# The residual stream kept by tokens: output and down projections into token tiles, norm sums along the free axis

## The chip, the cores and the metric

One core of one Trainium2 chip runs the kernel. The metric is the device time in microseconds (us); smaller is better. PE is TensorE, ACT ScalarE, DVE VectorE, POOL GpSimd and SP the engine that issues most of the DMAs.

## The reference

Two transformer blocks, one after the other, for one sequence of 256 tokens and 1024 features, all in float32. Cut to what the change touches:

```python
# first block
h = rms_norm(x, norm_mix_pre)
...                                   # attention and convolution of h @ w_in
mixed = g_a * y_a + g_c * y_c
x = x + rms_norm(mixed @ w_out, norm_mix_post)
h = rms_norm(x, norm_ffn_pre)
u = conv3(h @ w_up)                   # 1024 -> 2 x 2816
x = x + rms_norm((gelu(u_gate) * u_val) @ w_down, norm_ffn_post)
# second block
x = x + 0.5 * (silu(n @ w1) * (n @ w3)) @ w2      # n = rms_norm(x, ffn1_norm)
x = x + (gate_a * y_a + gate_b * y_b) @ w_out     # mixers of rms_norm(x, mix_norm) @ w_in
x = x + 0.5 * (silu(n @ w1) * (n @ w3)) @ w2      # n = rms_norm(x, ffn2_norm)
return rms_norm(x, final_norm)
```

rms_norm divides each token's 1024 features by the root of their mean square plus 1e-6 and multiplies them by a gain per feature.

## The kernel before

**Weight chunks.** All weight matrices are read once, in 172 chunks of 128 x 2048 floats (1 MB). A ring of three slots holds a chunk three times: raw as SP's DMA lands it, w_hi (ACT's rounding of raw to the format that PE multiplies in one pass, L1294) and w_lo (raw - w_hi, on POOL for chunks 1 to 25, L1244, on DVE for the others, L1721 and L1551). PE makes each product three times: w_hi x_hi, w_hi x_lo, w_lo x_hi (`three`, L1918). `split(n)` on ACT waits until chunk n has landed and chunk n-3 is used, so the split of a chunk can run only when PE has begun the one two before it.

**Layout.** x is held with features on the partitions, `x[128, 8, 256]`. `by_columns` (L1925) multiplies a chunk of 256 weight columns, as the stationary operand, by the whole of X: 8 blocks of features x 2 x 3 products of 256 tokens, into one PSUM bank. `by_rows` (L1954) takes a chunk of 256 weight rows (output and down projections), with weights stationary: 2 x 8 x 3 products of 256 tokens into four banks, output again by features. In the third feed-forward `rows_to_tokens` (L1975) does the same chunk with Y stationary and 512 weight columns moving: 2 x 4 x 3 products of 512 columns, into token tiles (t, h) of 128 tokens x 512 features; `x_to_tokens` (L1995) adds x to them by 32 products with the identity.

**Norms.** For a norm of x, ACT writes X_hi = x times gain (L1325) and DVE X_lo (L1573), so that PE can start on the unnormalised product; ACT squares x (L1300), PE sums the squares over the partitions by 32 products with one column (`sum_pair`, L2002, L2009), ACT takes the root (L1307), DVE the reciprocal and two diagonal matrices (L1560 to L1565), PE spreads them over the partitions at the fourth block of the layer's second chunk (`spread`, L2020), ACT copies them to rstd (L1316), and every evacuation of a bank multiplies by rstd (L1589, L1654). The two post-norms of the first block do the same with the output banks 4 to 7, with their sums inside the last chunk, multiply gained copies by the spread roots (L1597, L1604) and add to x (L1609). `residual` (L1617) adds a layer's output to x without a norm, pair of banks by pair.

**Order.** Each engine's program is written out by hand in one queue and waits on semaphores. Layers follow each other as: mixing of the first block (chunks A_...), feed-forward 0, feed-forward 1, the mixer of the second block (B0 ...), feed-forward 2. In a feed-forward (`feed`, L2029) PE takes a gate chunk, a value chunk and a down chunk in turn, 11 pairs and 11 down chunks. DVE's low part of the chunk after next stands behind the evacuations, and ahead of the norms at a layer's end. The first two chunks of a layer go to fresh banks; the third waits only for its w_lo.

Of the kernel before, what the change touches and what calls it, by code (L numbers as in the profile page):

```python
# [10 lines left out]
ALU = mybir.AluOpType  # L11
# [77 lines left out]
def block_pair(nc, inp, out, scratch, shifted):  # L89

    ctx = ExitStack()
    with ctx:
# [11 lines left out]
        x = sb("x", [P, NT, T])  # L104
# [3 lines left out]
        eps = sb("eps", [P, 4])  # L108
        rcol, rstd, diag = sb("rcol", [P, 4]), sb("rstd", [P, T]), sb("diag", [P, TT, P])
# [171 lines left out]
        LAYER_ENDS = (A_WO, A_END, ffn_at[1], B0, ffn_at[2], TOTAL)  # L281
# [21 lines left out]
        x_in = region(0, TT, D)  # L303
# [6 lines left out]
        final_gain = region(4096, D)  # L310
# [3 lines left out]
        gained = region(6144, 4, 2 * T)  # L314
# [106 lines left out]
        def pe_mixer(told, pe, state, by_columns, by_tokens, by_rows, sum_squares, spread):  # L421
            def columns(n, fresh=False, tokens=False, midway=None):
# [36 lines left out]
            columns(B0, fresh=True)  # L459
            sum_squares()  # L460
# [234 lines left out]
            for n in range(B_FP, ffn_at[2]):  # L695
# [4 lines left out]
                else:  # L700
                    r = n - B_WO
                    pe.wait_ge(S["mixed_lo"], 4 + r + 1)
                    by_rows(n, n % RING, 0, X_hi, X_lo, 2 * r, r == 0, r == 3, final=r == 3)


        def act_mixer(told, act, a, split, square, root, spread, state):
# [444 lines left out]
        def _(sp):  # L1151
# [15 lines left out]
            sp.dma_start(x_in, inp["x"].rearrange("a (t p) d -> p (a t) d", p=P)).then_inc(S["x_landed"], 16)  # L1167
# [8 lines left out]
            gain = inp["final_norm_2"]  # L1176
            for n in range(RING, TOTAL):
                load(n, n % RING, chunks[n])
                if n == ffn_at[2] + 12:
                    sp.dma_start(final_gain, bass.AP(gain.tensor, gain.offset, [[0, P], [1, D]])).then_inc(  # L1180
                        S["final_gain"], 16)
# [99 lines left out]
        def _(act):  # L1281
# [20 lines left out]
            def root(e):  # L1302


                a.activation(small[:, 61:62], ones[:, 0:1], ACT.Sqrt)
                act.wait_ge(S["sq_used"], 4 * state["norm"] + 4)
                a.activation(rcol[:, 2:4], bank[3][:, 256:258], ACT.Sqrt, bias=eps[:, e:e + 1],  # L1307
                             scale=1.0 / D).then_inc(S["column"], told.one("column"))
                act.wait_ge(S["column"], told.value("column"))
                state["norm"] += 1  # L1310
# [8 lines left out]
            def x_scaled(gain, ahead, first=False):  # L1319


                for p in range(4):
                    act.wait_ge(S["x_updated"], 4 * state["upd"] + p + 1)
                    for t in (2 * p, 2 * p + 1):
                        a.activation(X_hi[:, t, :], x[:, t, :], ACT.Copy, scale=col(gain, t)).then_inc(  # L1325
                            S["xg_hi"], told.one("xg_hi"))
                if first:
                    split(1)
                    act.wait_ge(S["constants"], 1)
                for p in range(4):  # L1330
                    square(p, flat(x[:, 2 * p:2 * p + 2, :]))
                state["upd"] += 1
                root(0)
                split(ahead)
                spread()

            def post_norm(last):

                for p in range(4):
                    if p < 3:  # L1340
                        act.wait_ge(S["pair_summed"], 3 * LAYER_ENDS.index(last) + p + 1)
                    else:
                        act.wait_ge(S["chunk_used"], last)
                    square(p, bank[4 + p][:, :])
                root(0)
                state["spread"] += 1
# [862 lines left out]
```

## Time and profile before

| | |
|---|---|
| median of 3 runs | 1256.07 us (1255.26 to 1256.3) |
| profiled execution | 1257.25 us, its span 1255.5 us |
| PE busy | 1197.8 us (95%) |
| DVE, ACT, POOL busy | 775.2, 551.0, 154.6 us |
| granted PE clock, mean | 0.962 |
| bytes moved | 187.97 MB, 150 GB/s |

The span is from the first to the last instruction of the profiled execution. The granted clock is the share of PE's full clock (2.4 GHz) that was allowed in a stretch. PE's queue is pipelined: a product starts before the one ahead of it has ended, so the distance between starts, not the duration, is its price in a stream.

### The profile page before, as it was taken

The page shows a single profiled execution, that of the slowest core. Times are in us where ns is not written, and L with a number is a line of the kernel's source. Part 1 is how long each engine was busy: PE and PEld are TensorE (multiplying, and loading weights), DVE is VectorE, ACT ScalarE, POOL GpSimd, SP SyncE. Part 2 cuts the span into 40 slices and gives each one's busy share as a digit, 9 for nine tenths or more (in the row PEclk, how much of TensorE's full clock was granted, in tenths as well). Part 3 has the DMA queues.
Part 4 walks back from the last instruction along what each step waited for, and adds up shares of the span by engine and source line. Part 5 has one row for each costly group of instructions (what it writes and reads, how often), then busy time and mean ns, then how long its engine had stood idle before and what let it go on. Part 6 is the DMA issues. An engine that isn't in the chain of part 4 may idle for free.

```text
span 1255.5 us, 23871 instructions
## 1 busy us (share of the span) xinstructions
PE 1197.8 (95%) x10503; PEld 1160.5 (92%) x10503; DVE 775.2 (62%) x1057; ACT 551.0 (44%) x613; POOL 154.6 (12%) x113
## 2 busy tenths in 40 slices
PE   6999999989899999989999998999899979999998
PEld 5999999989899999989999997989898879999997
DVE  3588976746587776765554566864266564555554
ACT  4433445473465554453433445523233354444343
POOL 3888770000000000000000000012000000000000
PEclk8999999999799999989999997999999989999999
DMA  6577553345155555526555543332032343565561
GB/s 210 167 233 240 170 168 132 113 146 174 51 184 186 193 175 169 199 65 203 169 169 194 172 151 104 115 103 84 22 101 91 112 134 102 168 210 171 172 199 67
DMA packets 143744, 187.97 MB, mean 150 GB/s; under 512 B 4384, under 2 KB 128857, under 8 KB 143661
## 3 DMA queue, kind: packets, MB, share of 16 engines
q1 hardware_dynamic: 142317, 183.22, 44.5%
q0 software_dynamic: 1104, 3.49, 0.8%
q8 instruction: 63, 1.03, 0.3%
q14 instruction: 20, 0.16, 0.0%
q10 hardware_dynamic: 240, 0.06, 0.0%
HBM read 185.70 MB, written 2.64 MB: 150 GB/s over the span
## 4 chain that ended last, share of the span: by engine, by line
PE 90%; DVE 5%; ACT 3%; issue 1%; ACTq 0%; DMA 0%; POOL 0%; DVEq 0%; POOLq 0%
PE bank L1921 24%; PE bank L1922 24%; PE bank L1923 24%; PE bank L536 2%; PE bank L2009 2%; PE bank L1987 2%; PE bank L1988 2%; PE bank L1989 2%; DVE w_lo L1551 1%; PE bank L596 1%; ACT w_hi L1294 1%; PE bank L2155 1%; DVE bank L1756 1%; PE bank L660 1%; PE bank L662 1%
## 5 line engine op out<-in xcount | busy, mean ns | idle before, releaser
L1921 PE MATMUL bank<-X_hi,w_hi 128*128 128x256 f32 x1968 | 572.3, 291 | 17.2 <-DVE X_lo L1573 11.7
L1922 PE MATMUL bank<-X_lo,w_hi 128*128 128x256 f32 x1968 | 567.3, 288 | 0.0
L1923 PE MATMUL bank<-X_hi,w_lo 128*128 128x256 f32 x1968 | 566.9, 288 | 0.0
L1921 PEld LDWEIGHTS bank<-X_hi,w_hi 128*128 128x128 f32 x1968 | 388.7, 197 | 22.4 <-issue 15.8
L1294 ACT ACTIVATE w_hi<-w_raw 128x2048 fp32r<-128x2048 f32 x172 | 328.5, 1911 | 178.0 <-PE bank L1923 164.8
L1922 PEld LDWEIGHTS bank<-X_lo,w_hi 128*128 128x128 f32 x1968 | 388.8, 198 | 0.4
L1923 PEld LDWEIGHTS bank<-X_hi,w_lo 128*128 128x128 f32 x1968 | 388.4, 197 | 0.0
L1551 DVE TENSOR_TENSOR w_lo<-w_raw,w_hi 128x2048 fp32r<-128x2048 f32 x146 | 333.8, 2287 | 84.1 <-ACT w_hi L1294 83.9
L1654 DVE TENSOR_TENSOR arena<-bank,rstd 128x512 f32<-128x512 f32 x66 | 45.7, 692 | 202.5 <-PE bank L1923 189.8
L1921 PE MATMUL bank<-Y_hi,w_hi 128*128 128x256 f32 x480 | 137.7, 287 | 2.3 <-DVE Y_lo L1103 1.4
L1922 PE MATMUL bank<-Y_lo,w_hi 128*128 128x256 f32 x480 | 136.8, 285 | 0.0
L1923 PE MATMUL bank<-Y_hi,w_lo 128*128 128x256 f32 x480 | 136.7, 285 | 0.0
L1244 POOL TENSOR_TENSOR w_lo<-w_raw,w_hi 128x2048 fp32r<-128x2048 f32 x25 | 116.0, 4647 | 39.3 <-ACT w_hi L1294 39.2
L1921 PEld LDWEIGHTS bank<-Y_hi,w_hi 128*128 128x128 f32 x480 | 93.2, 194 | 3.1 <-DVE Y_lo L1103 1.6
L1756 DVE SCALAR_TENSOR_TENSOR bank<-arena,par,bank 128x256 f32<-128x256 f32 x232 | 93.2, 486 | 0.6
L1922 PEld LDWEIGHTS bank<-Y_lo,w_hi 128*128 128x128 f32 x480 | 93.2, 194 | 0.0
L1923 PEld LDWEIGHTS bank<-Y_hi,w_lo 128*128 128x128 f32 x480 | 93.2, 194 | 0.0
L1275 POOL TENSOR_TENSOR arena<-arena,levels 128x512 f32<-128x512 f32 x10 | 12.7, 1279 | 622.8 <-DVE arena L997 589.2
L1366 ACT ACTIVATE arena<-arena,par 128x256 f32<-128x256 f32 x44 | 24.2, 599 | 71.8 <-DVE arena L1654 71.8
L1375 ACT ACTIVATE arena<-arena 128x512 f32<-128x512 f32 x22 | 14.0, 635 | 88.3 <-DVE arena L1654 88.3
L1589 DVE TENSOR_TENSOR arena<-bank,rstd 128x512 f32<-128x512 f32 x43 | 29.7, 690 | 36.4 <-PE bank L1923 32.4
L1389 ACT ACTIVATE Y_hi<-arena 128x512 fp32r<-128x512 f32 x33 | 20.9, 633 | 44.0 <-DVE arena L1679 25.0
(283 smaller groups left out, 1193.4 us busy)
## 6 DMA issues: line engine op xcount, KB each, us to landing
w_raw<-in_ffn_w_dram SPq DMA_DIRECT2D x66, 1024.0 KB, 5.3
w_raw<-in_w_in_dram SPq DMA_DIRECT2D x54, 1024.0 KB, 5.1
w_raw<-in_w_up_dram SPq DMA_DIRECT2D x22, 1024.0 KB, 5.1
w_raw<-in_w_down_dram SPq DMA_DIRECT2D x11, 1024.0 KB, 4.9
w_raw<-in_w_out_dram SPq DMA_DIRECT2D x8, 1024.0 KB, 4.9
w_raw<-in_conv_pw_w_dram SPq DMA_DIRECT2D x4, 1024.0 KB, 4.8
w_raw<-in_w_attn_out_dram SPq DMA_DIRECT2D x2, 1024.0 KB, 5.0
w_raw<-in_rwkv_proj_dram SPq DMA_DIRECT2D x2, 1024.0 KB, 5.0
```

The costliest lines, as they stand in the source:

```text
L536: mm = pe.matmul(head(bank[b], h, slice(i * CHUNK, (i + 1) * CHUNK)), left(f, i, h), right(f, i, h), start=True, stop=True)
L1244: g.tensor_tensor(w_lo[n % RING][:, :], raw[n % RING][:, :], w_hi[n % RING][:, :].bitcast(F32), ALU.subtract).then_inc(S["w_lo_pool"], tol ...
L1294: a.activation(w_hi[slot][:, :], raw[slot][:, :], ACT.Copy).then_inc(S["w_hi"], told.one("w_hi"))
L1551: v.tensor_tensor(w_lo[slot][:, :], raw[slot][:, :], w_hi[slot][:, :].bitcast(F32), ALU.subtract).then_inc(S["w_lo"], told.one("w_lo"))
L1589: v.tensor_tensor(dst, pairs(b), over(rstd[:], 2), ALU.mult).then_inc(S[f"bank{b}_read"], 1)
L1654: v.tensor_tensor(u_t[:, side].rearrange("p (m t) -> p m t", m=2), pairs(2 * (i % 2) + side), over(rstd[:], 2), ALU.mult).then_inc(S[name] ...
L1756: v.scalar_tensor_tensor(out=conv[:, t, :] if k == CONV_W - 1 else part, in0=src, scalar=w, in1=part, op0=ALU.mult, op1=ALU.add).then_inc( ...
L1921: pe.matmul(o, wh, xh, start=start, stop=False, skip_group_check=True)
L1922: pe.matmul(o, wh, xl, start=False, stop=False, skip_group_check=True)
L1923: return pe.matmul(o, wl, xh, start=False, stop=stop, skip_group_check=True)
L1987: pe.matmul(o, yh, wh, start=False, stop=False, skip_group_check=True)
L1988: pe.matmul(o, yl, wh, start=False, stop=False, skip_group_check=True)
```

## The change

x, the output of w_out and the down projections are held by tokens everywhere: `x[128 tokens, 2, 1024]`.

- All output and down projections use `rows_to_tokens`; `by_rows` stays for the attention, convolution and mixer projections. The last chunk of a layer goes tile by tile, before the two plain residuals with both token halves of feature half 0 first.
- Norm sums: ACT squares 512 features of 128 tokens with a sum along the free axis, adds the mean of half 0 as the bias of the root (`root_mean`). `sum_pair`, `sum_squares`, `x_to_tokens` and the DVE copies of the turned x at the start go.
- Post-norms: DVE multiplies a tile by the gain, which a DMA broadcasts over the partitions, and adds it to x scaled per token by the reciprocal root.
- For each norm of x, PE turns x by 16 transposes into four PSUM banks (`turned_place`), from where ACT and DVE make X_hi and X_lo. X_hi of a second block in a bank waits for X_lo of the first. Before the two plain residuals' followers 8 of the transposes stand inside the last chunk, and 8 ahead of the third block of the next chunk.
- At the end x gets its last residual on DVE, and the final norm is taken from it.

```diff
@@ turned_place @@
+        def turned_place(f, ends):
+            early, late = (2, 3), (4, 5)
+            if ends == B0:
+                early, late = (1, 3), (4, 6)
+            if ends in (0, ffn_at[2]):
+                early, late = (4, 5), (6, 7)
+            c = f % 4 // 2 * T
+            return bank[(early, late)[f // 4][f % 2]][:, c:c + T]
@@ SP @@
-            gain = inp["final_norm_2"]
+            gains = {A_WO: inp["norm_mix_post"][0, :], ffn_at[0] + 12: inp["norm_ffn_post"][0, :],
+                     ffn_at[2] + 12: inp["final_norm_2"]}
@@ ACT @@
+            def root_mean(t, halves, root, signal):
+                half, mean, whole = (stat[:, c + t:c + t + 1] for c in (0, 2, 4))
+                for h, (source, ready, count) in enumerate(halves):
+                    act.wait_ge(S[ready], count)
+                    a.activation(sq[:, h, :], source, ACT.Square, accum_out=half if h == 0 else whole).then_inc(
+                        S["half_squared"], told.one("half_squared"))
+                    act.wait_ge(S["half_squared"], told.value("half_squared"))
+                    if h == 0:
+                        a.activation(mean, half, ACT.Identity, bias=eps[:, 0:1], scale=1.0 / D).then_inc(
+                            S["act_step"], told.one("act_step"))
+                        act.wait_ge(S["act_step"], told.value("act_step"))
+                a.activation(root, whole, ACT.Sqrt, bias=mean, scale=1.0 / D).then_inc(S[signal], told.one(signal))
...
+            def high_part(f, gain, ends):
+                act.wait_ge(S["x_turned"], state["upd"] * NT + f // 4 * 4 + 2 * (f % 2) + 2)
+                if f % 4 >= 2:
+                    act.wait_ge(S["xg_lo"], state["upd"] * NT + f - 2 + 1)
+                a.activation(X_hi[:, f, :], turned_place(f, ends), ACT.Copy, scale=col(gain, f)).then_inc(
+                    S["xg_hi"], told.one("xg_hi"))
+            def x_scaled(gain, ends, ahead):
+                for f in range(NT):
+                    high_part(f, gain, ends)
+                first = 4 * state["upd"] - 4
+                for t in range(TT):
+                    token_root(t, lambda t, h: ("x_updated", first + (2 * h + t if ends in HALF_FIRST else 2 * t + h) + 1))
+                state["upd"] += 1
+                split(ahead)
+                spread()
...
             def post_norm(last):
+                root_table()
+                for t in range(TT):
+                    root_mean(t, [(bank[4 + 2 * t + h][:, :], *tile_ready(last, t, h)) for h in range(2)],
+                              stat[:, 6 + t:7 + t], "post_root")
@@ DVE @@
+            def post_norm(last, next_gain):
+                e = TOKEN_ENDS.index(last)
+                dve.wait_ge(S["gain_landed"], 16 * (e + 1))
+                for t in range(TT):
+                    for h in range(2):
+                        c = slice(512 * h, 512 * (h + 1))
+                        dve.wait_ge(S["half_squared"], 4 * state["squared"] + 2 * t + h + 1)
+                        v.tensor_tensor(gained[:, t, c], bank[4 + 2 * t + h][:, :], token_gain[:, c], ALU.mult).then_inc(
+                            S["y_gained"], told.one("y_gained"))
+                    dve.wait_ge(S["post_root"], 2 * e + t + 1)
+                    v.reciprocal(stat[:, 8 + t:9 + t], stat[:, 6 + t:7 + t]).then_inc(
...
+                    for h in range(2):
+                        c = slice(512 * h, 512 * (h + 1))
+                        v.scalar_tensor_tensor(out=x[:, t, c], in0=gained[:, t, c], scalar=stat[:, 8 + t:9 + t],
+                                               in1=x[:, t, c], op0=ALU.mult, op1=ALU.add).then_inc(
+                            S["x_updated"], told.one("x_updated"))
+                for f in range(NT):
+                    low_part(f, next_gain, last)
+                x_norm()
+            def residual(last, scale, next_gain, base=4):
+                residual_tile(last, scale, 0, 0, base)
+                residual_tile(last, scale, 1, 0, base)
+                low_part(0, next_gain, last)
+                low_part(1, next_gain, last)
+                residual_tile(last, scale, 0, 1, base)
+                low_part(2, next_gain, last)
+                low_part(3, next_gain, last)
+                residual_tile(last, scale, 1, 1, base)
+                for f in range(4, NT):
+                    low_part(f, next_gain, last)
+                x_norm()
@@ PE @@
+            def by_bank(h):
+                return [4 * h + f for f in (0, 2, 1, 3)]
+            def turn_early_half(ends):
+                pe.wait_ge(S["x_updated"], 4 * TOKEN_ENDS.index(ends) + 2)
+                turn_half(0, ends)
+            def turn_late_half():
+                if state["ends"] in HALF_FIRST:
+                    pe.wait_ge(S["x_updated"], 4 * TOKEN_ENDS.index(state["ends"]) + 4)
+                    turn_half(1, state["ends"])
+            def turn_by_tokens(ends):
+                before = 4 * TOKEN_ENDS.index(ends)
+                for h in range(2):
+                    pe.wait_ge(S["x_updated"], before + h + 1)
+                    for f in by_bank(h):
+                        turn(f, 0, ends)
+                for h in range(2):
+                    pe.wait_ge(S["x_updated"], before + 2 + h + 1)
+                    for f in by_bank(h):
+                        turn(f, 1, ends).then_inc(S["x_turned"], told.one("x_turned"))
@@ PE, rows_to_tokens @@
+                if ends in HALF_FIRST:
+                    tiles = [(t, h) for h in range(2) for t in range(TT)]
...
+                    if last and at < 7:
+                        mm.then_inc(S["tile_summed"], told.one("tile_summed"))
+                    if ends in HALF_FIRST and at == 5:
+                        turn_early_half(ends)
@@ PE, feed @@
-                by_columns(b0, b0 % RING, 0, fresh=True)
-                sum_squares()
+                by_columns(b0, b0 % RING, 0, fresh=turn_late_half)
                 by_columns(b0 + 1, (b0 + 1) % RING, 1, midway=spread)
-                if k == 2:
-                    x_to_tokens()
```

HALF_FIRST is (B0, ffn_at[2]), the two plain residuals inside the net; `fresh()` is called ahead of the third block.

## Rows read from the trace of the kernel before

**Rows 1.** The page: chain of work that ended last, by engine

```profile
PE 90%; DVE 5%; ACT 3%; issue 1%; ACTq 0%; DMA 0%; POOL 0%; DVEq 0%; POOLq 0%
```

**Rows 2.** Timeline of PE, feed-forward 0: start us, duration us, engine, line, tiles

```profile
497.31 0.28 PE L1921 MATMUL bank<-Y_hi,w_hi 128*128 128x256 f32 x1
...
503.07 0.28 PE L1921 MATMUL bank<-X_hi,w_hi 128*128 128x256 f32 x1
```

**Rows 3.** Timeline of PE, feed-forward 2: first products of a down and the next chunk

```profile
1221.93 0.40 PE L1987 MATMUL bank<-w_hi,Y_hi 128*128 128x512 f32 x1
...
1227.39 0.28 PE L1921 MATMUL bank<-X_hi,w_hi 128*128 128x256 f32 x1
```

**Rows 4.** Windows, steady feed-forwards: stretch, length, each engine's busy us, PEclk, DMA

```profile
344.00:521.00 177.00, 176.51 (x1469) 176.30 (x1468) 131.88 (x163) 95.34 (x100) 0.00 (x0) 1.00 0.56 184
1067.00:1250.00 183.00, 182.98 (x1287) 172.11 (x1285) 99.67 (x80) 76.32 (x65) 0.00 (x0) 1.00 0.50 164
```

**Rows 5.** Windows of the start and the layer boundaries: PE, PEld, DVE, ACT, POOL, PEclk

```profile
23.79:38.60 14.81, 14.81 (x97) 12.42 (x96) 2.54 (x8) 5.64 (x5) 5.65 (x2) 0.77 0.43 142
312.22:347.55 35.33, 30.36 (x219) 30.11 (x217) 18.90 (x35) 16.68 (x27) 0.00 (x0) 0.81 0.17 59
521.45:556.58 35.13, 30.15 (x216) 29.76 (x216) 20.64 (x34) 15.59 (x27) 0.00 (x0) 0.81 0.18 61
729.55:750.16 20.61, 20.03 (x169) 19.83 (x168) 11.44 (x21) 11.60 (x18) 0.00 (x0) 1.00 0.33 103
1045.75:1074.49 28.74, 28.16 (x214) 27.97 (x213) 14.78 (x21) 17.12 (x22) 0.00 (x0) 0.88 0.32 102
```

**Rows 6.** Timeline of PE: first product of feed-forward 0's last down chunk

```profile
521.45 0.38 PE L1921 MATMUL bank<-Y_hi,w_hi 128*128 128x256 f32 x1 [0.95 <-DVE Y_lo L1686]
```

**Rows 7.** Groups of instructions of PE by line and form: busy us, mean ns, idle

```profile
L2009 PE MATMUL bank<-ones,sq 128*128 128x1 f32 x224 | 26.7, 251 | 0.0
...
L455 PE MATMUL bank<-ident,arena 128*128 128x128 f32 x32 | 4.1, 272 | 0.0
...
L1999 PE MATMUL bank<-ident,x 128*128 128x128 f32 x32 | 3.7, 275 | 0.0
```

**Rows 8.** Timeline of POOL, then of PE, at the start

```profile
18.30 4.72 POOL L1244 TENSOR_TENSOR w_lo<-w_raw,w_hi 128x2048 fp32r<-128x2048 f32 x1 [9.40 <-ACT w_hi L1294]
...
28.25 2.72 PE L2099 MATMUL bank<-arena 32*4 32x256 f32 x6
```

**Rows 9.** Chain of work from 520 to 560, and PE's timeline at 537

```profile
529.90 1.28 ACT L1305
...
545.48 3.47 PE bank L2009 x32
...
537.18 0.55 PE L1921 MATMUL bank<-X_hi,w_hi 128*128 128x256 f32 x1 [3.64 <-DVE X_lo L1573]
```

**Rows 10.** Timeline of ACT and PE at the end: final norm

```profile
1245.93 0.60 ACT L1520 ACTIVATE sq<-bank 128x512 f32<-128x512 f32 x1 [3.23 <-PE bank L1989]
...
1246.66 0.30 ACT L1523 ACTIVATE small<-small,eps 128x1 f32<-128x1 f32 x1
...
1248.02 0.30 ACT L1530 ACTIVATE small<-small 128x1 f32<-128x1 f32 x1
...
1249.59 0.39 PE L1989 MATMUL bank<-w_lo,Y_hi 128*128 128x512 f32 x1
...
1250.94 1.32 ACT L1536 ACTIVATE arena<-arena,rcol 128x512 f32<-128x512 f32 x2
```

**Rows 11.** Timeline of ACT before the mixer: X_hi from x

```profile
738.45 0.92 ACT L1325 ACTIVATE X_hi<-x,par 128x256 fp32r<-128x256 f32 x2 [0.60 <-DVE x L1625]
```

**Rows 12.** Timeline of DVE before the mixer: low part, residual, X_lo

```profile
731.76 2.29 DVE L1551 TENSOR_TENSOR w_lo<-w_raw,w_hi 128x2048 fp32r<-128x2048 f32 x1 [2.28 <-ACT w_hi L1294]
733.97 1.41 DVE L1625 SCALAR_TENSOR_TENSOR x<-bank,x 128x512 f32<-128x512 f32 x2
735.41 0.88 DVE L1573 SCALAR_TENSOR_TENSOR X_lo<-x,par,X_hi 128x256 fp32r<-128x256 f32 x2
```

More of the change, by code:

```diff
@@ L1615, in post_norm @@
[L1615 to L1632 removed]
+                    dve.wait_ge(S["y_gained"], told.value("y_gained"))
@@ L1905, in _ @@
             told = Count()
-            state = {"norm": 0, "xg": 0, "diagonals": 0, "rstd": 0, "ffn": 0}
-            AFTER_PAIRS = (8, 12)
+            state = {"norm": 0, "xg": 0, "diagonals": 0, "rstd": 0, "ffn": 0, "ends": 0}
             def split_ready(n):
@@ L1984, in rows_to_tokens @@
                     c = k * D + 512 * h
-                    yh, yl = (y[:, k0 + k, t * P:(t + 1) * P] for y in (Y_hi, Y_lo))
+                    yh, yl = (y[:, k0 + k, t * P:(t + 1) * P] for y in (hi, lo))
                     wh, wl = (w[slot][:, c:c + 512] for w in (w_hi, w_lo))
-                    pe.matmul(o, yh, wh, start=False, stop=False, skip_group_check=True)
+                    last = ends is not None and k == 1
+                    pe.matmul(o, yh, wh, start=first and k == 0, stop=False, skip_group_check=True)
@@ L1988, in rows_to_tokens @@
                     pe.matmul(o, yl, wh, start=False, stop=False, skip_group_check=True)
-                    mm = pe.matmul(o, yh, wl, start=False, stop=last and k == 1, skip_group_check=True)
-                    if last and k == 1:
-                        mm.then_inc(S["tokens_summed"], told.one("tokens_summed"))
-                if not last:
-                    mm.then_inc(S["chunk_used"], told.one("chunk_used"))
-            def x_to_tokens():
-                for t in range(TT):
-                    for f in range(NT):
-                        pe.matmul(bank[4 + 2 * t + f // 4][:, f % 4 * P:f % 4 * P + P], x[:, f, t * P:(t + 1) * P],
-                                  ident[:], start=f % 4 == 0, stop=False, skip_group_check=True)
@@ L2002, in sum_pair @@
-            def sum_pair(p):
-                if p == 0 and state["rstd"] > 0:
-                    pe.wait_ge(S["rstd"], state["rstd"])
-                pe.wait_ge(S["sq_ready"], 4 * state["norm"] + p + 1)
-                for m in range(2):
-                    for t in range(TT):
-                        mm = pe.matmul(bank[3][:, 256 + t:257 + t], sq[:, p, m * T + t * P:m * T + t * P + P],
-                                       ones[:, 0:1], start=p == 0 and m == 0 and t == 0,
-                                       stop=p == 3 and m == 1, skip_group_check=True)
-                mm.then_inc(S["sq_used"], told.one("sq_used"))
-                state["norm"] += p == 3
@@ L2015, in sum_squares @@
-            def sum_squares():
-                for p in range(4):
-                    sum_pair(p)
+                    mm = pe.matmul(o, yh, wl, start=False, stop=last, skip_group_check=True)
+                    if last and at < 7:
+                        mm.then_inc(S["tile_summed"], told.one("tile_summed"))
+                    if ends in HALF_FIRST and at == 5:
+                        turn_early_half(ends)
+                mm.then_inc(S["chunk_used"], told.one("chunk_used"))
+                if ends is not None:
+                    state["ends"] = ends
```

282 lines of the change are left out of this document (111 added, 171 removed).

## The prediction, made before the changed kernel was run

> **What bounds the kernel now.** The chain of the work that ended last comes first: 90% of the span is TensorE [rows 1]. So a microsecond is worth what it is worth on PE's queue, in PE work removed, in PE waits, or in PE's clock. In the timeline of PE a 256-wide row chunk (48 products) of the first feed-forward takes 503.07 - 497.31 = 5.76 us, 120 ns a product [rows 2]. The third feed-forward already makes its down projection by tokens, 24 products of 512 columns: 1227.39 - 1221.93 = 5.46 us, 227.5 ns each [rows 3]. The windows of the steady stretches show PE without gaps and at the full clock, with DVE at 75% or less [rows 4]. The windows of the boundaries between layers are where the rest lies: from the start of a layer's last chunk to the start of the third chunk of the next, 35.33 and 35.13 us pass at the two post-norms, 28.74 us before the third feed-forward, and the start spends 14.81 us between chunk 0 and chunk 2, at clocks of 0.77 to 0.88 [rows 5]. Three chunks need 17.3 us, so these four stretches hold some 60 us that are not weight products.
>
> **1. Wide products.** 11 + 11 down chunks and 4 + 4 output chunks go from 5.76 to 5.46 us, 0.30 each. Outside the boundaries (part 3) there are 10 + 10 + 3 + 3 = 26. One of them, the one before the last of the first feed-forward, gains nothing: PE waits after it for Y_lo anyway [rows 6]. 25 x 0.30 = 7.5 us. The steady work of ScalarE and VectorE stays as it is and was already hidden at the shorter period in the third feed-forward [rows 4]. The trace's other end is the duration of a wide product alone, 0.40 us [rows 3]; it is the slower rival. The Trainium skill (TensorE: Matmul & The Clock Gate, "Back-to-back issue gap") gives N/2.4 + 2.5 ns for the pace of a matmul in a stream: 109 and 216 ns, so a chunk would save 0.06 us and the whole part 1.5 us. The rows show 120 and 227.5 ns, a toll of about 13 ns per product, and I go by the rows.
>
> **2. Start.** Seven sets of 32 one-column sums are in the trace (224 products, 26.7 us as durations) [rows 7]. The first stands between chunk 0 and the parameter transposes and is gone: 3.6 us. What is late next: ScalarE now squares by tokens, so its split of chunk 2 ends near 28.2, and POOL's low part takes 4.7 us [rows 8], so chunk 2 can't start before 32.8. The six table products run at 0.43 us each [rows 8], behind the sums at half rate. If the clock stays up, PE is there at 31.6 and waits for POOL; if it falls as now, chunk 2 starts at 34.6. Before it was 38.6 (the window's end) [rows 5]. Gain 4.0 to 5.8, taken 4.8 us.
>
> **3. The two post-norms**, worked for the second, from S = 521.45, the start of the last down chunk [rows 6]. Tiles are ready at S+1.4, 2.7, 4.1, 5.45. ScalarE: split until 1.05, Sqrt table (1.28 us [rows 9]) and dummy until 2.55, then squares of 0.73 us start to start of the mean, 0.3 for the mean and 0.3 for the root [rows 10], 2.05 us a token: tokens done at 4.65 and 6.65. DVE: its weight low part ends at 4.35; then 4 gains of PSUM, 4 updates at 0.61 to 0.7 each and two reciprocals, in order: half 3 of x at 9.3, half 4 at 9.85. Then a transpose pair on PE (0.45), X_hi (0.46 [rows 11]), X_lo (0.44 to 0.5 [rows 12]): PE restarts at S+10.9. Now it restarts at 537.18 [rows 9], S+15.7: spread matmuls, the copy through PSUM and the sums inside the last chunk are gone. X_hi and X_lo alternate by bank but need 0.45 us each per block against PE's 0.72, so PE is not starved. Chunk 0 ends at 16.65. On SBUF x the norm follows X_hi: 13.5 + 4.1 = 17.6 for the root, 18.5 for the diagonals, and PE arrives for the spread at 18.8, so the sums (3.47 us [rows 9]) are gone without a new wait. The weight split behind the root, the rstd copy, the evacuation and a DVE low part of 2.29 [rows 12] give 22.9; PE is free at 22.8. Third chunk at S+23.0, if the clock is full. Now it falls: 0.81 over 35.13 us is 13.3 us at half rate (1.2 of 2.4 GHz) [rows 5]. Half rate costs at most half of PE's busy time in it; with a denser PE queue, one short of half rate left, I add 1.8 (bounds 0 and 6). 35.1 - 24.8 = 10.3 us. The first post-norm has ScalarE's split 1 us later, 35.3 - 25.1 = 10.2 us.
>
> **4. Before the mixer**, from S = 729.55. New: PE waits inside the last chunk. DVE's weight low part ends at 734.05, S+4.5, then the first two tiles of the residual [rows 12]: x half ready at S+5.75, while PE has reached the wait at S+4.1. Behind it stand 8 transposes, the fourth tile (1.36), then chunk B0, whose third block waits again for x at S+9.9 and for 8 more transposes (0.9). Chunk B0 ends at S+15.1 (now, sums included, 15.9). ScalarE's X_hi ends at 12.5, two tokens of norm 16.65, diagonals 17.55, spread 18.0. The weight split and low part end at 20.95 against S+20.6 now [rows 5]. The mixer's first chain starts there, so nothing is gained: +0.3 us (bounds -1 and +2).
>
> **5. Before the third feed-forward** the same schedule, but PE goes on: third chunk at S+22.0 instead of 28.74 [rows 5]: -6.7 us. Of that, 32 matmuls that moved x into tokens (3.7 us) and the sums are the whole [rows 7].
>
> **6. Tail.** Now the last product starts at 1249.59 and the last scaling ends at 1250.94 + 1.32 = 1252.26, 2.3 us after PE's end near 1249.98 [rows 10]. After, every tile has an update and a gain on DVE (1.4 us against 1.36 of PE), squares wait for the update: end at PE's end + 4.4. +2.0 us.
>
> **Covered.** X_hi and X_lo now read PSUM; evacuations show about the same durations. Two more gain broadcasts of 512 KB go through SP's queue; the one in the third feed-forward today leaves PE busy 182.98 of 183 us [rows 4]. If that cover failed, each costs half a weight load, some 2.5 us. At the start X_hi waits for X_lo by bank, which pushes ScalarE's split of chunk 1 back by 2.3 us; POOL's low part of it then ends at 25.3 instead of 23.0 [rows 8], when PE is just done with transposes and tables. If PE waits there, it is for less than 1 us, and POOL's next part is the later bound anyway.
>
> **Sum.** -7.5 - 4.8 - 10.3 - 10.2 + 0.3 - 6.7 + 2.0 = -37.2 us. Against the profiled execution, 1257.25 us (span 1255.5), that is 1220.05; it stood 1.2 us above the median of 1256.07, so the median becomes 1218.9, say **1219 us**.
>
> **Rivals.**
> *The clock falls at every boundary.* For it: all boundaries show it now [rows 5], and transposes fill a part of the queue. Against: one-column sums precede most of the falls, and the mixer's 32 transposes took 4.1 us together without a lasting fall [rows 7]. A full half-rate stretch more at each of five boundaries, 1.8 us each beyond mine: 1228. Here a rule of the Trainium skill speaks against the change: in "Part 4: PE-mode transpose" (same page) transposes don't count as PE work for the clock. By it the 16 at each boundary would keep the clock down. Chance 0.17.
> *The clock stays up.* 1.8 + 1.7 at the post-norms and 0.8 at the start come on top: 1215. Chance 0.11.
> *ScalarE's norm becomes the wait.* Its 4.1 us stand ahead of the weight split of the third chunk, with margins of 0.1 to 0.3 us. If every step is 30% longer or hangs on DVE, 2 us at five places: 1229. Chance 0.09.
> *The wide product gains nothing* (1219 + 7.5 = 1226.5). Only the page's pace speaks for it. Chance 0.02.
> *Slower.* In the first three layers the wide products stand beside other work; were they paced by their own duration, 24 x 0.40 = 9.6 us a chunk, 30 chunks would cost 115 us more, less the 29.7 of the other parts: 1341. It decides from a pace of 0.28 us, where 30 chunks x (24 x 0.28 - 5.76) eats those 29.7. Against it: the third feed-forward runs such products all through its gapless window [rows 3, 4]. Chance 0.03.
> *It doesn't do what it says*: sums or the old layout stay somewhere, each set 3.5 us: 1223 to 1233; nothing in the diff shows it. Chance 0.02.
>
> **Numbers.** The forecast has 0.56. The range reaches up over the clock and the norm rivals and the bound of part 4, and down over a full clock and a margin of 6 us for rows rounded in my favour or not: 1209 to 1232. No change within 0.2% (2.5 us, about what a measurement of this kernel can tell from none) lies 35 us away; it needs two rivals at once or much of the last one: 0.01. Slower 0.03, faster 0.96.
>
> **What would show it.** Right: no one-column products; 5.45 us for every down chunk; restarts 5 to 6 us after a post-norm's last product, third chunks 23 to 25 us after S; a PE wait of 1.7 us inside the last chunk at the two residuals; clock near 0.9 in the boundary windows; mixer entry unmoved. Wrong: a pace above 0.24 us, PE waits for w_lo or diagonals over 1 us at the third chunks, or half rate from the transposes on.

## The result, and the profile after

The changed kernel takes 1218.66 us (median of 4 runs, 1216.44 to 1220.1) against 1255.66 us beside it: a ratio of 0.9704, 95% interval 0.9687 to 0.9721, so 37.0 us faster. The forecast was 1219.0. In two later groups of runs the same kernel gave 1218.62 and 1218.75 us, with ratios of 0.9691 (0.9675 to 0.9708) and 0.9687 (0.9672 to 0.9702); the kernel before gave 1258.24 and 1257.57 us beside it, so the gain was 39.6 and 38.8 us there. The profiled execution is the quickest of its four, 1216.44 us with a span of 1214.5; that of the kernel before, 1257.25 us, stands 1.6 us above the 1255.66, so the spans differ by 41.0 us and the medians by 37.0.

The page of the changed kernel: busy time by engine, the granted clock in 40 slices, and the chain that ended last.

```profile
PE 1154.7 (95%) x9583; PEld 1085.6 (89%) x9583; DVE 769.8 (63%) x1039; ACT 558.7 (46%) x660; POOL 154.5 (13%) x113
...
PEclk8999999989999999999999987999999989999999
...
PE 85%; DVE 7%; ACT 5%; issue 1%; ACTq 1%; POOL 0%; DMA 0%; DVEq 0%; POOLq 0%
```

PE has 85% of the chain instead of 90 [rows 1], and VectorE and ScalarE have 12% instead of 8: the norms were shortened less than PE's own work. The bound is the same.

Windows of the changed kernel, for the same five stretches as [rows 5]: end of chunk 0 to start of chunk 2, then from the start of a layer's last chunk to the start of the third chunk of the next (at the mixer to the end of its second; the mixer's row of [rows 5] ends 1.6 us earlier than that, at 750.16, where VectorE starts to read the first chunk, so the two rows aren't to be subtracted). Columns as there: stretch, length, busy time of PE, PEld, DVE, ACT, POOL, clock, DMA share, GB/s.

```profile
23.06:32.20 9.14, 8.37 (x64) 7.03 (x63) 3.21 (x9) 7.84 (x13) 6.44 (x3) 1.00 0.35 117
306.21:330.55 24.34, 21.57 (x141) 19.27 (x139) 14.75 (x25) 18.60 (x40) 0.00 (x0) 0.93 0.26 87
501.83:525.57 23.74, 21.61 (x140) 19.46 (x140) 16.82 (x25) 17.93 (x40) 0.00 (x0) 0.93 0.25 89
695.47:717.47 22.00, 20.02 (x141) 18.11 (x139) 12.64 (x24) 13.02 (x25) 0.00 (x0) 1.00 0.30 96
1009.56:1031.35 21.79, 19.96 (x141) 18.09 (x139) 11.82 (x19) 15.14 (x28) 0.00 (x0) 1.00 0.29 97
```

In the two post-norms PE does 8.8 and 8.5 us less work than in [rows 5], the length falls by 11.0 and 11.4 us, and the clock rises from 0.81 to 0.93. Two profiles more of the same kernel agree with these lengths to 0.1 us, but for the start (8.2 and 9.1 us, where chunk 0 ends up to 1.4 us later).

PE's waits in the changed kernel: line, who was waited for, us in total, times, longest.

```profile
PE bank L476 <- ACT arena L730: 5.6, 1, 5.6
PE bank L2007 <- DVE x L1640: 4.9, 4, 1.4
PE bank L2190 <- ACT arena L1509: 4.5, 4, 3.6
PE bank L2007 <- DVE x L1656: 3.5, 4, 1.5
...
PE bank L2062 <- DVE Y_lo L1722: 1.2, 1, 1.2
```

The wait of 3.64 us for X_lo at each post-norm [rows 9] is replaced by short ones for halves of x (L1640), and the residual tiles (L1656) have brought the wait of 1.5 us inside the last chunk. The wait before the mixer's first small products (L476) grew from 4.82 us to 5.58.

The terms, as spans of the two profiles between the same points, the start of a chunk's last product (part 4 to the mixer's first small product, part 6 to the end of the span):

| Part | forecast | measured |
|---|---|---|
| 1. wide products | -7.5 | -8.1 (-1.0, -3.1, -3.1, -0.9) |
| 2. start | -4.8 | -6.2 |
| 3. second post-norm, first post-norm | -10.3, -10.2 | -11.1, -10.8 |
| 4. before the mixer | +0.3 | +0.5 |
| 5. before the third feed-forward | -6.7 | -6.8 |
| 6. tail | +2.0 | +2.2 |
| attention of the first mixer, second mixer (clock) | 0 | +1.05, -1.75 |
| sum | -37.2 | -41.0 |

### The profile page after: what moved, and what is told of

The parts are those of the page before. It is cut to its first block, busy times and chain, and to the rows that moved or that the text cites. A ratio compares the mean times of both kernels' runs of the same rounds, so it can differ in the third digit from the quotient of the medians.

```text
span 1214.5 us, 22068 instructions
## 1 busy us (share of the span) xinstructions
PE 1154.7 (95%) x9583; PEld 1085.6 (89%) x9583; DVE 769.8 (63%) x1039; ACT 558.7 (46%) x660; POOL 154.5 (13%) x113
## 4 chain that ended last, share of the span: by engine, by line
PE 85%; DVE 7%; ACT 5%; issue 1%; ACTq 1%; POOL 0%; DMA 0%; DVEq 0%; POOLq 0%
PE bank L1954 20%; PE bank L1955 19%; PE bank L1956 19%; PE bank L2062 5%; PE bank L2063 5%; PE bank L2064 5%; PE bank L546 2%; DVE w_lo L1582 2%; ACT w_hi L1306 2%; PE bank L606 1%; ACT sq L1320 1%; PE bank L2190 1%; DVE bank L1788 1%; PE bank L670 1%; PE bank L672 1%
## 5 line engine op out<-in xcount | busy, mean ns | idle before, releaser
L1954 PE MATMUL bank<-X_hi,w_hi 128*128 128x256 f32 x1840 | 527.8, 287 | 4.0 <-DVE X_lo L1603 3.2
L1955 PE MATMUL bank<-X_lo,w_hi 128*128 128x256 f32 x1840 | 523.9, 285 | 0.0
L1956 PE MATMUL bank<-X_hi,w_lo 128*128 128x256 f32 x1840 | 523.7, 285 | 0.0
L1955 PEld LDWEIGHTS bank<-X_lo,w_hi 128*128 128x128 f32 x1840 | 356.5, 194 | 1.2
L2062 PE MATMUL bank<-w_hi,Y_hi 128*128 128x512 f32 x264 | 103.3, 391 | 1.2 <-DVE Y_lo L1722 1.2
L2063 PE MATMUL bank<-w_hi,Y_lo 128*128 128x512 f32 x264 | 103.1, 390 | 0.0
L2064 PE MATMUL bank<-w_lo,Y_hi 128*128 128x512 f32 x264 | 102.7, 389 | 0.0
L2062 PEld LDWEIGHTS bank<-w_hi,Y_hi 128*128 128x128 f32 x264 | 49.7, 188 | 11.2 <-DVE Y_lo L1722 1.6
L2064 PEld LDWEIGHTS bank<-w_lo,Y_hi 128*128 128x128 f32 x264 | 49.6, 188 | 10.5
L2063 PEld LDWEIGHTS bank<-w_hi,Y_lo 128*128 128x128 f32 x264 | 49.7, 188 | 9.1
```

Source lines behind the costliest of these rows:

```text
L1954: pe.matmul(o, wh, xh, start=start, stop=False, skip_group_check=True)
L1955: pe.matmul(o, wh, xl, start=False, stop=False, skip_group_check=True)
L1956: return pe.matmul(o, wl, xh, start=False, stop=stop, skip_group_check=True)
L2062: pe.matmul(o, yh, wh, start=first and k == 0, stop=False, skip_group_check=True)
L2063: pe.matmul(o, yl, wh, start=False, stop=False, skip_group_check=True)
L2064: mm = pe.matmul(o, yh, wl, start=False, stop=last, skip_group_check=True)
```

## The experiments

Each edit is made to the changed kernel. The tables that the readings rest on are the times between the ends of the same numbered chunks; chunk 42 ends where the last output chunk begins, 46 is the third of the first feed-forward, 111 is the mixer's second, 113 its fourth. Durations of steady stretches agree to 0.01 us between profiles, so a difference there is the edit's.

### The changed kernel again

> The changed kernel once more, beside the others on one chip: 1218.7 us and a ratio of 0.970 to the kernel before by every theory. Its time is what the other runs of this group are compared with.

> The changed kernel beside the three others of this group, to show how far its median moves between groups: 1218.6 us, a ratio of 0.969 to 0.970.

1218.62 and 1218.75 us. The three profiles differ most at the second mixer, chunk 119 to 134: 196.55, 198.73 and 198.76 us, with 10.2, 13.7 and 13.7 us of it at half rate. Smaller differences stand in the first mixer's attention (chunk 26 to 39: 110.65, 109.55 and 110.71 us, with 6.8, 3.4 and 6.8 us at half rate), from chunk 134 to 137 (21.7, 22.5 and 22.6 us) and at the start (chunk 2 ends within 0.4 us). Over all kernels below, with the same work there, this stretch took 195.6 to 204.9 us with 10.2 to 27.3 us at half rate. It is why I read single parts from the profiles and not from whole times, which it moves by up to 6 us. What decides it stays open.

### Narrow products

```diff
-pe.matmul(o, yh, wh, ...); pe.matmul(o, yl, wh, ...)
-mm = pe.matmul(o, yh, wl, ...)
+for q in range(2):
+    r = slice(256 * q, 256 * q + 256)
+    pe.matmul(o[:, r], yh, wh[:, r], ...); pe.matmul(o[:, r], yl, wh[:, r], ...)
+    mm = pe.matmul(o[:, r], yh, wl[:, r], ...)
```

> Every 512-column product of the output and down projections becomes two of 256 columns, 48 a chunk instead of 24, the rest unchanged. 41 chunks have them, some two of them beside a PE wait. My step 1 (120 against 227.5 ns a product, 0.30 us a chunk): 39 x 0.30 = 11.7 us slower than the changed kernel, about 1230. The page's pace (0.06 us a chunk): 2.3 us slower, 1221.

1227.02 us against 1218.62 in the same group (ratio to before 0.9767, 0.9751 to 0.9784). The same 28 chunks of the first feed-forward, 9 of them wide, in the changed kernel and then in the narrow one:

```profile
336.28:494.86 158.58, 158.58 (x1130) 149.95 (x1129) 118.67 (x145) 83.61 (x86) 0.00 (x0) 1.00 0.57 191
```

```profile
339.77:501.05 161.28, 161.28 (x1346) 161.28 (x1345) 119.05 (x144) 82.94 (x86) 0.00 (x0) 1.00 0.57 187
```

PE is busy throughout in both, at the full clock: 2.70 us over 9 chunks, 0.30 each, as the rows of before had it. The Trainium skill (TensorE: Matmul & The Clock Gate, "Back-to-back issue gap") gives N/2.4 + 2.5 ns, 109 and 216 ns, for an isolated product, and 131 ns for products of 512 columns in a sustained stream of weight loads and products; step 1 took the first for the pace in a stream. Neither fits here: the trace has 120 and 227.5 ns, and the 0.06 us a chunk of the isolated product isn't met. The weight loads show the other side: PEld is 94.6% busy with wide products and 100% with narrow ones. All three feed-forwards give the same 2.70 over the same 28 chunks. The median rose by 8.4 instead of 11.7 us; in the profiles the stretch from chunk 113 to 134 took 4.7 us less than in the changed kernel beside it, with 6.9 us less at half rate, which is more than the 3.3 that are missing.

### The sums back

```diff
 if fresh:
     state["xg"] += 1
+    for k in range(NT):
+        for t in range(TT):
+            pe.matmul(bank[3][:, 256 + t:257 + t], x[:, t, k * P:(k + 1) * P],
+                      ident[:, 0:1], ...)
```

> Sixteen fp32 one-column products (32 records) stand again after the first chunk of each of the five layers; nothing reads their result. If the gain at the boundaries is the PE time that they took, each set costs 3.5 us at the two post-norms and before the third feed-forward (10.5), 2 to 3 at the start, 0 to 1.4 at the mixer, where PE waits anyway: 13 to 15 us, 1232 to 1234. If these products, and not the wait before them, are also what let the clock fall, half-rate stretches come back behind them at the start and the post-norms, each of 6.8 us worth 3.4 us: up to 10 us more, 1235 to 1243, with the third chunks at the post-norms back near S+28. If the clock falls for the waits at each boundary alone, its stretches stay as in the changed kernel.

1243.24 us (0.9884, 0.9869 to 0.9899), 24.6 us more than the changed kernel and just past the upper case. In the windows of this kernel, chunk 0 to 2 and chunk 43 to 46, then of the changed one for the second:

```profile
24.08:44.69 20.61, 20.61 (x144) 18.52 (x143) 5.71 (x10) 9.65 (x12) 12.14 (x4) 0.83 0.36 111
317.03:348.63 31.60, 28.84 (x198) 27.42 (x196) 17.61 (x32) 18.04 (x39) 0.00 (x0) 0.84 0.22 68
```

```profile
311.42:336.28 24.86, 22.09 (x165) 20.68 (x164) 17.58 (x32) 18.03 (x39) 0.00 (x0) 0.93 0.27 86
```

At the start and at the first post-norm the sums cost 6.6 and 6.75 us, of which 3.5 are the products and the rest 6.8 us more at half rate, beginning at 28.4, behind the sums that ended at 27.8, and at 332.2, inside them. At the second post-norm it is 3.7 us, with no more half rate; before the third feed-forward 4.7, with 3.4 us of it; from chunk 108 to 113, over the mixer's first wait, 0.7. That makes 22.4 us at the five places. So most of what the change gained at the boundaries is the sums, their PE time first and the clock behind them second. At the start PE has no wait between the chunks (20.61 of 20.61 us busy), so there the clock fell without one, behind the one-column products. That the clock fell also in the second mixer (27.3 us from chunk 119 to 134) isn't explained.

### Turns as plain products

```diff
-return pe.transpose(turned_place(f, ends)[...], x[...], ident[:])
+return pe.matmul(turned_place(f, ends)[...], x[...], ident[:], start=True, stop=True)
```

> The 16 turns of x at each layer are made by an fp32 matrix product with the identity instead of a transpose; place and data are the same. The trace of before priced 16 such products at 3.7 us against some 1.9 for 16 transposes, so at most 1.8 us more at each of five boundaries, of which the halves that PE has time for (it waits for DVE there) cost nothing: 3 to 6 us slower, 1222 to 1225. If transposes do not count for the clock and matrix products do, as the page has it, the half-rate stretches after them go (58 us of the changed kernel's span are at half rate, five boundaries hold most of it), which gives back up to 3.4 us a boundary: 1208 to 1220, and the clock above 0.976. If the clock does not tell them apart, it stays at 0.976.

1221.27 us (0.9701, 0.9682 to 0.9719), 2.65 us more, the clock 0.978 in both profiles. Both residual boundaries took 1.91 us more, the price of 16 fp32 products over 16 transposes. The two post-norms took 0.67 and 0.46 us less, without their 3.4 us at half rate; but another kernel below, with the transposes, also had none there. The 1208 to 1220 us and the higher clock that were expected by the Trainium skill's rule on transposes ("Part 4: PE-mode transpose" of the page named above) did not come. But the changed kernel has half rate at only two of the five places, 3.4 us each, so there was little to give back, and this run alone doesn't settle the rule.

### The early turns later

```diff
-if ends in HALF_FIRST and at == 5:
+if ends in HALF_FIRST and at == 7:
```

> At the two residuals (before the mixer and before the third feed-forward) the first eight turns of x come after the fourth tile of the last chunk instead of before it, so PE has the fourth tile's 1.36 us of products to make while it waited 1.51 and 0.24 us for x. My step 4: the mixer's start hangs on ScalarE's and VectorE's chain, so this wait costs nothing and nothing is gained there, at the third feed-forward 0 to 0.3: the time of the changed kernel, a ratio to before of 0.969 within 0.001. The rival, that a PE wait inside a chunk is time of the span: 1.5 to 1.8 us faster.

1220.50 us (0.9702, 0.9683 to 0.9721). From chunk 108 to 111 21.95 us pass and from 137 to 141 27.75, in both kernels. So where the turns stand makes no difference. That isn't yet a wait that costs nothing: at both places PE's waits for x are not gone but moved, 0.15, 0.74 (for X_lo) and 0.66 us instead of 1.51 and 0.24. At the mixer the small products wait for ScalarE afterwards, 5.58 us in both kernels, so nothing of it reaches them; at the third feed-forward no other wait of PE follows, and 1.5 of the 21.8 us are VectorE's residual. In the profiles the second mixer took 3.4 us more than in the changed kernel (202.1 us, 20.5 at half rate), which is more than the 1.9 us between the medians.

### One more square

```diff
+if h == 1:
+    a.activation(sq[:, 0, :], sq[:, 0, :], ACT.Square)
 a.activation(sq[:, h, :], source, ACT.Square, accum_out=...)
```

> ScalarE makes one more square of 512 columns (0.73 us) per token in every norm: 2 at the start, 4 at each post-norm layer, 2 at each of the two residuals, 4 at the end, its result unused. If ScalarE's norm stands on the path as my working has it (margins of 0.1 to 0.3 us at the third chunks): 1.2 to 1.5 us more in the post-norm itself and again in the norm of x, so about 2.5 at each post-norm, 1.5 at the mixer, 1.2 at the third feed-forward, 1.5 at the end, nothing at the start where POOL is later: 9 us slower, 1228. If the margins are larger than I worked out, only the post-norms and the end pay: 4 to 5 us.

1226.32 us (0.9761, 0.9734 to 0.9787), 7.7 us slower by the medians but only 3.1 between the profiles; the profiled execution is the quickest of its five. ScalarE at the start, each token's first square, in the changed kernel and then in this one:

```profile
21.50 0.61 ACT L1320 ACTIVATE sq<-x 128x512 f32<-128x512 f32 x1
...
23.53 0.61 ACT L1320 ACTIVATE sq<-x 128x512 f32<-128x512 f32 x1
```

```profile
21.79 0.61 ACT L1322 ACTIVATE sq<-x 128x512 f32<-128x512 f32 x1
...
24.33 0.61 ACT L1322 ACTIVATE sq<-x 128x512 f32<-128x512 f32 x1
```

A token takes 2.54 us instead of 2.03, so a square lengthened the norm by 0.51 us and not by the 0.73 that I had put down, 1.0 us for two tokens. By stretch: start +0.9 (where I had expected nothing; but POOL's low part waits for ScalarE's split, and that stands behind the squares: it starts at 28.85, in two profiles of the changed kernel at 27.52 and 27.93), first post-norm +1.5 (with 3.4 us more at half rate), second +0.3 (3.4 less), mixer +0.76, third feed-forward +1.03, end +1.07. Every norm is on the path: where the clock was the same, 1.0 us of squares cost 0.8 to 1.1, so the margins are 0 to 0.3 us, about what I had. At the post-norms, with two norms each and so 2.0 us of squares, less of it arrived, and the clock hides how much. What the medians have more than the profiles isn't located.

### The mixer's first chain ahead of the weights

```diff
-split(B0 + 2)
 out_bank(B0, lora_in[:, :, 1:T + 1])
...
 dve.wait_ge(S["lora_shifted"], told.value("lora_shifted"))
+split(B0 + 2)
```

and on ScalarE, for this layer alone, `spread()` before `split(ahead)`.

> At the mixer's start alone, ScalarE copies the spread before it splits the next weights, and VectorE reads chunk B0 and makes the mixer's first inputs before its low part of the same weights. In the changed kernel the spread is there at 713.2 and the copy waits for the split until 714.1, then the low part (2.3 us) stands before the reading. If that chain is what sets the first products of the mixer (PE waits 5.6 us for it), they come 2.5 to 3 us earlier, and the chunk behind them has its low part by then: 2 to 3 us faster, 1216. If the weights split later are the next wait, nothing is gained or up to 1 us lost.

1216.57 us (0.9681, 0.9662 to 0.9701). ScalarE and VectorE of the changed kernel, around the mixer's start:

```profile
712.30 1.90 ACT L1306 ACTIVATE w_hi<-w_raw 128x2048 fp32r<-128x2048 f32 x1
714.10 0.36 ACT L1350 ACTIVATE rstd<-bank 128x256 f32<-128x256 f32 x1
719.03 1.28 ACT L726 ACT_TABLE_LOAD   x1 [4.56 <-DVE arena L885]
```

```profile
714.30 2.29 DVE L1582 TENSOR_TENSOR w_lo<-w_raw,w_hi 128x2048 fp32r<-128x2048 f32 x1 [0.66 <-ACT w_hi L1306]
716.51 0.68 DVE L1619 TENSOR_TENSOR arena<-bank,rstd 128x512 f32<-128x512 f32 x1
```

and ScalarE of this kernel:

```profile
713.07 0.39 ACT L1350 ACTIVATE rstd<-bank 128x256 f32<-128x256 f32 x1 [1.52 <-PE bank L2083]
713.49 1.92 ACT L1306 ACTIVATE w_hi<-w_raw 128x2048 fp32r<-128x2048 f32 x1
715.42 1.28 ACT L726 ACT_TABLE_LOAD   x1
```

The reading of the first chunk no longer stands behind the low part of the weights. PE's wait before the small products falls from 5.58 us to 2.82, and 20.5 us instead of 24.68 pass from chunk 111 to 113:

```profile
716.34:736.84 20.50, 17.68 (x114) 16.51 (x113) 15.10 (x21) 11.51 (x17) 0.00 (x0) 0.83 0.49 154
```

2.8 us of it come by the chain and the rest with 3.4 us less at half rate. By the medians of the two groups 2.1 us are left of it, as the second mixer again took longer (202.3 us).

### Filling the mixer's wait: products, transposes, both edits

```diff
+for _ in range(40):
+    pe.matmul(bank[7][:, 0:T], Y_hi[:, 0, 0:P], Y_hi[:, 0, :], start=True, stop=True)
 pe.wait_ge(S["lora_landed"], 64)
 pe.wait_ge(S["lora_act"], 3)
```

In the second kernel these lines are `pe.transpose(bank[7][:, 0:P], x[:, 0, 0:P], ident[:])`; in the third, 22 of the products stand beside the edit above.

> Forty products of 256 columns, unused (4.8 us at 120 ns), fill most of PE's 5.6 us wait before the mixer's first small products; nothing else moves. In the changed kernel 10.2 us at half rate follow this wait (722.5 to 732.7) and as many again from 746. If the idle wait brings the clock down, the stretch behind it goes, and the chunk and small products there run in some 4 us less (the kernel with the sums back had 3.4 us less at half rate there and was 3.9 us shorter between the same chunks): 3 to 4 us faster, 1215. If the clock falls for the small products themselves, or on its own, nothing changes.

> The place of the forty products in PE's wait before the mixer's first small products is taken by forty transposes of x into a bank that nothing reads (110 to 117 ns each, 4.4 to 4.7 us). If transposes don't count as work for the clock, as the page has it, this wait is as idle as before: 10.2 us at half rate behind it, and 24.7 us from chunk 111 to chunk 113, the changed kernel's time. If they count like products, there is no half rate there and 20.2 us pass between these chunks, as with the forty products: 3.5 to 4.5 us faster.

> The mixer's chain first, and 22 unused products (2.6 us) in what is left of PE's wait there (2.82 us). If the two gains are separate, the earlier chain (2.8 us) and the full clock behind the wait (4.5 us) add up: 17.4 us between chunks 111 and 113, 7 us faster than the changed kernel, 1211.5. If the earlier chain's gain was mostly the clock's, the sum is no more than the forty products gave: 20 us there and 1214.9.

With products 1214.89 us (0.9665, 0.9647 to 0.9683), with transposes 1214.61 (0.9655, 0.964 to 0.967), with both edits 1212.57 (0.964, 0.9624 to 0.9656). The windows from chunk 111 to 113: the changed kernel, then with products, with transposes, and with both edits.

```profile
717.19:741.87 24.68, 19.10 (x114) 17.52 (x113) 14.73 (x24) 12.44 (x17) 0.00 (x0) 0.79 0.39 128
```

```profile
715.82:736.03 20.21, 19.43 (x155) 18.67 (x153) 14.42 (x23) 12.12 (x17) 0.00 (x0) 1.00 0.50 156
```

```profile
716.51:738.21 21.70, 20.49 (x155) 19.68 (x154) 14.74 (x24) 12.34 (x17) 0.00 (x0) 0.92 0.46 146
```

```profile
717.75:735.22 17.47, 17.28 (x136) 16.52 (x135) 14.80 (x21) 11.21 (x17) 0.00 (x0) 1.00 0.58 181
```

In the changed kernel PE idles for 5.58 us and then runs at 1.2 GHz for 10.2 us, from 722.45. With 40 unused products in the wait (0.78 us of it left) there is no half rate, and 4.5 us are saved without anything on the path being earlier. So the idle wait is what this fall came from. The transposes, in PE's timeline of that kernel:

```profile
716.64 4.53 PE L474 MATMUL bank<-ident,x 128*128 128x128 f32 x40
722.38 1.31 PE L478 MATMUL bank<-arena 32*128 32x256 f32 x5 [1.21 <-ACT arena L732]
```

They cut the half rate from 10.2 to 3.4 us, though 1.21 us of the wait stayed open. By the rule of the Trainium skill (TensorE: Matmul & The Clock Gate, "Part 4: PE-mode transpose") transposes don't count as PE work for the clock in the same way, and the 10.2 us should have stayed. They didn't: here fp32 transposes kept the clock up, for the most part. (In the seven profiles that leave this wait whole and empty, 10.2 to 13.7 us stand at half rate from chunk 111 to 113.) Whether they do so fully isn't settled by this pair.

The two edits add up as expected, 17.47 us between the chunks (forecast 17.4).

### All the fillings

On top of the kernel with both edits; the added products are told in words.

```diff
+if it == UNITS - 1:
+    27 unused products of X_hi into bank 3
 pe.wait_ge(S["pT_ready"], it + 1)
...
+8 unused products of Y_hi into bank 0
 for h in range(2):
     pe.wait_ge(S["x_updated"], before + h + 1)
...
+10 unused products
 for h in range(2):
     pe.wait_ge(S["x_updated"], before + 2 + h + 1)
```

> As the one with the mixer's chain first and 22 products, and 27 more unused products in PE's wait of 3.65 us in the last unit of the first mixer's attention (6.8 us at half rate begin in it) and 8 + 10 in its two waits of 0.7 to 1.4 us inside each post-norm (3.4 us at half rate behind each). If an idle PE is what the clock falls for, these stretches go too: 2 to 3 us at the attention and 0.5 to 1 at each post-norm, 1208 us. If the small products around them bring it down, nothing more is gained, 1211.5; and where the 8 products are later than x, up to 0.3 us is lost at each post-norm.

1206.56 us (1204.13 to 1208.41; 0.9595, 0.9579 to 0.961), 12.2 us faster than the changed kernel beside it and the fastest of the study. The two profiles differ by 13.3 us: 7.2 from chunk 111 to 113, 2.65 at the attention, 1.8 at the post-norms, and 1.7 at the second mixer, where nothing was edited. The first post-norm, chunk 43 to 46, to be held against the changed kernel's 24.86 us and 0.93 above:

```profile
308.96:332.88 23.92, 22.99 (x184) 21.76 (x183) 17.61 (x32) 18.04 (x39) 0.00 (x0) 1.00 0.28 90
```

From chunk 26 to 39 108.06 us pass instead of 110.65 (110.71 and 109.55 in the other profiles of the changed kernel), with no half rate there; at the post-norms 23.91 and 23.34 instead of 24.86 and 24.13. The kernel with 40 products had the same two values at the post-norms without an edit there, so that part may be chance; the attention's 1.5 to 2.6 us are not met in any profile of the plain changed kernel, though the kernel with plain turns had 108.03 once.

## Why the prediction was right

**Step 1 (wide products) held.** 0.30 us a chunk in three feed-forwards, and 0.30 given back by narrow products. The chunk before the last of the first feed-forward gained nothing, as written: the wait for Y_lo rose from 0.95 to 1.22 us. The 0.6 us by which the measured -8.1 exceeds 7.5 lies mostly in how stretches are cut between this step and its neighbours: each of the four ends with a wide chunk, whose last product starts 0.1 us earlier before its end, and one holds that chunk. The slower rival (0.40 us a product) and the one without a gain fall with the same windows.

**Step 2 (start) was too small**, -6.2 against -4.8 and bounds of 4.0 to 5.8 (-5.8 and -6.1 with the other two profiles of the changed kernel). The mechanism is as written: chunk 2 starts at 32.20 after a wait of 0.77 us for POOL's low part, for which I had 32.8. What I weighed half is the clock: without the sums the 6.8 us at half rate are gone whole, in all three profiles, and they come back with the sums.

**Step 3 (post-norms) held, for the reasons given, but for the size of the clock's part.** ScalarE and VectorE in the second post-norm of the changed kernel, S = 501.83:

```profile
502.81 1.28 ACT L1344 ACT_TABLE_LOAD   x1
504.10 0.20 ACT L1344 ACTIVATE small<-ones 128x1 f32<-128x1 f32 x1
504.21 0.58 ACT L1320 ACTIVATE sq<-bank 128x512 f32<-128x512 f32 x1
...
508.38 0.29 ACT L1327 ACTIVATE stat<-stat 128x1 f32<-128x1 f32 x1
```

```profile
506.10 1.28 DVE L1631 TENSOR_TENSOR arena<-bank,arena 128x512 f32<-128x512 f32 x2
507.30 0.15 DVE L1634 RECIPROCAL stat<-stat 128x1 f32<-128x1 f32 x1
507.48 1.42 DVE L1640 SCALAR_TENSOR_TENSOR x<-arena,stat,x 128x512 f32<-128x512 f32 x2
...
510.20 1.42 DVE L1640 SCALAR_TENSOR_TENSOR x<-arena,stat,x 128x512 f32<-128x512 f32 x2
```

The second token's root is there at S+6.8 (6.65 written), x whole at S+9.8 (9.85), PE's first product of the next layer at 512.87, S+11.0 (10.9), its third chunk at S+23.7 (23.0). The 0.7 us over the 23.0 are about what the 3.4 us at half rate cost: the kernel with 40 products had none there and was 0.8 us shorter. 1.8 had been added for it (24.8), and that allowance is the main reason why the gain came out above 10.3.

**Step 4 held**: the mixer's small products come 27.58 us after S instead of 27.16, and the wait inside the last chunk (1.51 us, written 1.7) is there; moving the turns left this time as it was. **Step 5 held** to 0.1 us in its size. Its account of what the gain consists of is incomplete: it named the 32 matmuls and the sums as the whole, but 6.8 us at half rate went too (clock 0.88 in [rows 5], 1.00 here), and of the 4.7 us that the sums bring back there some 1.2 come with 3.4 us at half rate. **Step 6 held**: the last product ends near 1206.85 and the last scaling at 1211.06, 4.2 us later (4.4 written). ScalarE at the end of the changed kernel:

```profile
1209.54 0.29 ACT L1327 ACTIVATE stat<-stat 128x1 f32<-128x1 f32 x1
1209.74 1.32 ACT L1567 ACTIVATE arena<-arena,stat 128x512 f32<-128x512 f32 x2
```

**The rivals.** The clock didn't fall at every boundary: of the five windows above, those of the two post-norms alone have half rate, 3.4 us each. It didn't stay up either. The Trainium skill's rule on transposes, which spoke for more, isn't borne out. ScalarE's norm is on the path, as the extra square shows, but it wasn't longer than worked out (2.03 us a token, written 2.05).

**What the sum had right by luck.** The median fell by 37.0 and the sum said 37.2, yet the terms of the profiles give 41.0, and the six parts alone 40.3 where 37.2 was written: the start, the two post-norms and the wide products each gave 0.6 to 1.4 us more. The attention's 1.05 us and the second mixer's 1.75, which no step had, are within what those stretches scatter. 3.8 us are where the two profiled executions stand to their medians (2.2 below, 1.6 above). With the 39.6 and 38.8 us of the later groups, the change is worth some 2 us more than the sum said, and the agreement to 0.2 us is luck.

## What to carry to other kernels

Price a PE queue by the pace between starts in a gapless window of the same kernel, not by an instruction's duration: 24 products of 512 columns took 5.46 us though each shows 0.39. Small one-column products between layers cost twice, their own 3.5 us and up to 3.3 us of half clock behind them; sums along the free axis moved to ScalarE cost neither here, though they stand on the path with at most 0.3 us of room. And PE's wait of 5.6 us before the mixer's products cost its own length and the half clock after it, so an order that shortens such a wait, or work that fills it, can gain more than the wait's share of the path suggests.

## What the runs showed of the hardware that I had not expected

- Unused products in a wait make the kernel faster: 40 of them (4.96 us) before the mixer's small products saved 4.5 us behind them, and 85 in six waits, with the reordering, 12.2 us of 1218.75.
- Forty fp32 transposes in the same wait took 109 ns each from start to start and left 3.4 of 10.2 us at half rate.
- The same work in the second mixer ran 10.2 to 27.3 us at half rate and took 195.6 to 204.9 us from one kernel to the next, one profile of each. For a change worth 2 us, that scatter can hide it in a median of five.
